# Where a skewed weight unit begins: 128 and 192 bytes behind a multiple of 256 in place of 64

## The reference

```python
for l in range(DEPTH):                       # first block
    proj = x @ w_in[l]                       # 1024 x 8200
    # retention, and an mLSTM on convolved q and k, each gated and projected
    mix = (gate_a * y_ret + gate_b * y_ml) @ w_out[l]
    x = _layer_norm(DEEPNORM_ALPHA * x + mix, ln1_g[l], ln1_b[l])
    gu = x @ w_gate_up[l]                    # 1024 x 5632
    hidden = jax.nn.silu(gu[..., :D_FF]) * gu[..., D_FF:]
    x = _layer_norm(DEEPNORM_ALPHA * x + hidden @ w_down[l], ln2_g[l], ln2_b[l])
for l in range(DEPTH):                       # second block
    proj = rms_norm(x) @ w_in_2[l]           # 1024 x 3584
    # dilated attention, a gated linear recurrence, stick-breaking attention
    x = x + y @ w_out_2[l]
```

## Time and profile before

| | |
|---|---|
| median of 3 runs | 1157.38 us (1156.76 to 1159.45) |
| profiled execution, its time | 1157.0 us |
| profiled execution, its span | 1155.2 us |
| TensorE busy with matmuls | 1142.6 us, 99% |
| VectorE, ScalarE busy | 67%, 50% |
| mean DMA rate | 183 GB/s |
| clock granted to TensorE in the 40 slices of the page | full in all |

### The profile page before, as it was taken

One profiled execution on the slowest core, in us unless ns is written; L12 is line 12 of the kernel. 1 busy time (PEld: TensorE's weight loads), 2 busy tenths in 40 slices (PEclk: granted clock), 3 DMA queues, 4 the chain that ended last, 5 costly groups with the idle time before them and its releaser, 6 DMA issues.

```text
span 1155.2 us, 18539 instructions
## 1 busy us (share of the span) xinstructions
PE 1142.6 (99%) x7762; PEld 1039.4 (90%) x7762; DVE 772.9 (67%) x1056; ACT 577.2 (50%) x668; POOL 28.8 (2%) x36
## 2 busy tenths in 40 slices
PE   9999999999999999999999999999999999999997
PEld 7989998998999988999998898899988789978996
DVE  5887866667655546697774667755555766885676
ACT  6565445433544434454544544444443456745663
POOL 0000000001000000000000000000000100010000
PEclk9999999999999999999999999999999999999999
DMA  8764455556656463745455556765556363346320
GB/s 298 272 218 147 163 202 175 191 184 210 223 186 214 162 206 113 249 152 183 140 189 182 183 183 218 232 206 179 187 201 216 139 219 124 133 146 245 128 93 37
DMA packets 130098, 211.62 MB, mean 183 GB/s; under 512 B 6624, under 2 KB 52704, under 8 KB 129888
## 3 DMA queue, kind: packets, MB, share of 16 engines
q1 hardware_dynamic: 128272, 204.15, 52.5%
q0 software_dynamic: 1744, 6.29, 1.7%
HBM read 209.37 MB, written 1.05 MB: 182 GB/s over the span
## 4 chain that ended last, share of the span: by engine, by line
PE 89%; ACT 4%; DVE 3%; issue 2%; DMA 1%; SPq 1%; POOL 0%; POOLq 0%; DVEq 0%; ACTq 0%
PE ps L513 87%; DMA raw<-in_w_in 1%; ACT wh L999 1%; DVE wl L1430 1%; PE ps L740 1%; PE ps L646 1%; PE ps L840 0%; ACT L1038 0%; SPq L447 0%; POOL small L468 0%; ACT L1041 0%; DVE xl L1524 0%; ACT ee L1317 0%; PE ps L822 0%; DVE zz L1996 0%
## 5 line engine op out<-in xcount | busy, mean ns | idle before, releaser
L1430 DVE TENSOR_TENSOR wl<-raw,wh 128x2048 fp32r<-128x2048 f32 (+1 forms) x186 | 415.0, 2237 | 167.0 <-ACT wh L999 166.7
L999 ACT ACTIVATE wh<-raw 128x2048 fp32r<-128x2048 f32 (+1 forms) x190 | 358.4, 1892 | 184.3 <-PE ps L513 162.4
L513 PE MATMUL ps<-xh,wh 128*128 128x256 f32 x1328 | 370.4, 279 | 1.5 <-issue 1.5
L513 PE MATMUL ps<-xl,wh 128*128 128x256 f32 x1328 | 367.2, 277 | 0.0
L513 PE MATMUL ps<-xh,wl 128*128 128x256 f32 x1312 | 363.4, 277 | 0.0
L513 PEld LDWEIGHTS ps<-xh,wh 128*128 128x128 f32 x1328 | 249.7, 188 | 4.7 <-issue 4.1
L513 PEld LDWEIGHTS ps<-xl,wh 128*128 128x128 f32 x1328 | 249.9, 188 | 0.2
L513 PEld LDWEIGHTS ps<-xh,wl 128*128 128x128 f32 x1312 | 246.7, 188 | 0.0
L513 PE MATMUL ps<-wh,xh 128*128 128x512 f32 (+1 forms) x440 | 171.4, 390 | 2.6 <-DVE xl L1524 1.6
L513 PE MATMUL ps<-wh,xl 128*128 128x512 f32 (+1 forms) x440 | 168.3, 383 | 0.0
L513 PE MATMUL ps<-wl,xh 128*128 128x512 f32 (+1 forms) x440 | 168.1, 382 | 0.0
(11 more groups left out here) (303 smaller groups left out, 1471.8 us busy)
## 6 DMA issues: line engine op xcount, KB each, us to landing
raw<-in_w_in SPq DMA_DIRECT2D x89, 1024.0 KB, 4.9
raw<-in_w_gate_up SPq DMA_DIRECT2D x88, 512.0 KB, 4.8
raw<-in_w_down SPq DMA_DIRECT2D x20, 1024.0 KB, 4.8
raw<-in_w_out SPq DMA_DIRECT2D x16, 1024.0 KB, 4.8
raw<-in_w_proj_ret SPq DMA_DIRECT2D x8, 1024.0 KB, 4.8
raw<-in_w_proj_mlstm SPq DMA_DIRECT2D x8, 1024.0 KB, 4.8
rows<-in_ln_g POOLq DMA_DIRECT2D x4, 512.0 KB, 4.2
rows<-in_ln_b POOLq DMA_DIRECT2D x4, 512.0 KB, 5.7
```

What stands on the lines that cost most here:

```text
L513: return pe.matmul(o, a, b, start=start, stop=False, skip_group_check=True)
L999: act.activation(stretch(wh, u, 0, m), source(u)[:, 0:m], ACT.Copy).then_inc(s_hi, 1)
L1430: dve.tensor_tensor(stretch(wl, u, a, nk * n), source(u)[:, a:nk * n], f32(stretch(wh, u, a, nk * n)), ALU.subtract).then_inc(s_lo, 1 if a ...
```

## The change

The constant `APART = (32, 48)` gives a skew for each layer. Every unit that was skewed by 16 floats (64 bytes) is skewed by 32 floats (128 bytes) in layer 0 and by 48 floats (192 bytes) in layer 1, in both blocks. Column 3072 of `w_in_2`, which is the unit of cvg, had no skew and gets the same one. Nothing else differs: no instruction, wait, transfer or buffer is added or moved.

```diff
+APART = (32, 48)
...
         for c0 in (3072, 3584, 1024, 1536, 0, 512, 6152, 6664, 7176, 7688, 2048, 2560, 5120, 5632):
-            cols(w, c0, 512, SKEW if c0 in (3072, 3584, 0, 512, 6152, 6664, 7176, 7688) else 0)
-        for name, skew in (("w_proj_ret", SKEW), ("w_proj_mlstm", SKEW), ("w_out", 0)):
+            cols(w, c0, 512, APART[l] if c0 in (3072, 3584, 0, 512, 6152, 6664, 7176, 7688) else 0)
+        for name, skew in (("w_proj_ret", APART[l]), ("w_proj_mlstm", APART[l]), ("w_out", 0)):
...
-                                      (g[:, k0:k0 + KU, FF + 256 * j:FF + 256 * j + 256], 256, 256)], SKEW if j > 1 else 0))
+                                      (g[:, k0:k0 + KU, FF + 256 * j:FF + 256 * j + 256], 256, 256)], APART[l] if j > 1 else 0))
...
         for c0 in (0, 512, 1024, 1536, 2560, 2048, 3072):
-            cols(A["w_in_2"][l], c0, 512, SKEW if c0 in (1536, 2560, 2048) else 0)
+            cols(A["w_in_2"][l], c0, 512, APART[l] if c0 in (1536, 2560, 2048, 3072) else 0)
```

## The result

The changed kernel took 1175.37 us (median of 4 runs, 1175.06 to 1175.65) beside 1157.42 us for the kernel before in the same runs. The ratio is 1.0155, 95% interval 1.0143 to 1.0167. The forecast was 1156.2 us with a range of 1153.3 to 1166.0, so the time lies above the range, and it moved the other way than forecast.

A forecast was written before the change was run, and what follows sets the result against it. The prediction took TensorE to bound the kernel, as matmul count by step from start to start. Its four terms, -1.2 + 0 + 0 + 0 us, took the median 1157.4 to 1156.2 us, range 1153.3 to 1166.0.

The forecast's parts named there:

- the floor: Fastest steady step of 256-column matmuls on TensorE, 113.3 ns from start to start, which no skew was to lower.
- Step (1): Skewed 256-column stages: half of 522 slow steps near 117.8 ns return to 113.3 ns, -1.2 us.
- the catches: Stretches of skewed matmuls entered at a slow pace of 117.8 ns that then holds; 522 steps, 2.3 us in all.
- The bounds of (1): Pace of the skewed stages: the floor of 113.3 ns from below, the unskewed 120.0 ns from above.
- The rival with both layers caught: Every skewed step of both layers at 117.8 ns, 1175 us; part of a rival with chance 0.18.
- Step (2): First few slow steps behind each interruption of skewed stages: 0 forecast, at best -0.7 us.
- Step (3): cvg's newly skewed unit: 1.25 us less TensorE work, hidden by ScalarE and VectorE work, so 0 forecast.
- Step (4): ScalarE and VectorE on shifted slots: L1430 2291 to 2295 ns skewed, 2282 unskewed; 0 forecast.
- The catch spreads: Skewed steps go to 117.8 ns: 7.9 us in block one for one layer, 1166.3 us total; chance 0.18.
- 128 as bad as 0: Pattern repeats at 128 bytes, so layer 0 runs at 120.0 ns throughout, 1171.3 us; chance 0.12.
- Everything pays: All slow stretches and slow beginnings go and cvg's saving is exposed, 1153.1 us; chance 0.10.
- Nothing happens: Distance matters only as zero or not zero, with cvg's saving hidden, 1157.4 us; chance 0.10.

## Why the prediction was wrong, step by step

**The bound and the floor: right.** No stretch in any of the fourteen kernels ran below 113.3 ns, and all 18 us came through the step.

**Step (1), the skewed stages: wrong, and it alone decides.** It put the catches at -1.2 us, "half of them gone", "because the step from 0 to 64 bytes took the pace from always 120 to mostly 113.3, and a larger distance needs a larger slip". That made a direction out of two points. Measured: 18.2 us more in place of 1.2 less. The pace isn't monotone in the distance; 80 bytes is already slow, and of the distances tried only 64 and 192 were ever seen at 113.3 ns, 64 in most stretches and 192 in few. What was right in it is that a pace "belongs to how a stretch is entered, and it then holds"; the step stopped short of asking which distances have a free pace to enter at all (128 has none) and which have one but seldom find it (192).

**The bounds of (1): right, the range wrong.** All steady paces that were measured lie between 113.3 and 120.0 ns. The rival with both layers caught gave 1175 us, which is the time measured, but in part by luck: layer 0 of the first block cost 2.0 us more than the 7.9 it had (a pace of 118.7 and not 117.8 ns), and layer 1 cost 1.4 us less (free stretches). The range stopped at one layer, on the ground that "nine tenths escape now". That counts escapes at 64 bytes only and says nothing of 128 or 192. With two distances that no row showed, both ends belonged in the range.

**Step (2), beginnings: can't be read apart** after the change, since most stages no longer reach the floor. **Step (3), cvg hidden: right**, shown by the run with cvg alone (ratio 1.0001, wait for yl 0.2 to 0.9 us) and by the chain's 29.39 us before and after. The mechanism that I gave, side work of ScalarE and VectorE, is what the chain shows. **Step (4), L1430: right**, 2293 ns. But its reading was not: the 2282 ns is that of `wls`, a spare buffer that one unit alone uses, and the other unskewed units of that window have a median of 2292 ns, so skew made no difference that this line shows. The skewed units are 100, not some 120. In the kernel before:

```profile
L1430 DVE TENSOR_TENSOR wl<-raw,wh x9: 1224/2292/2293, 850.6 to 888.7; 128x2048 fp32r<-128x2048 f32 x8, 128x1024 fp32r<-128x1024 f32 x1
```

**The rivals.** *The catch spreads*, which had a chance of 0.18, was the right one in place and near in size: 7.9 us forecast for a layer at 117.8 ns, 6.5 measured in layer 1, where some stretches stayed free, and 9.9 in layer 0, where the pace is 118.7. *128 as bad as 0* is wrong in its ground, a period of 128 bytes: 192 did not behave like 64, and the long stretch at 128 has 118.7 ns; that some stretches at 128 have 120.0 ns it had right. *Everything pays* is wrong: no catch was saved, and cvg's saving stayed hidden. *Nothing happens* is wrong: the step is up to 6.7 ns longer than 113.3 by distance alone. The Trainium skill (TensorE: Matmul & The Clock Gate, Part 2: What happens when you issue a matmul) says that loading the next weights takes no SBUF read bandwidth from the running matmul. That all distances would then be alike does not agree with the runs; whether it is read bandwidth that the 6.7 ns go to, no run here shows.

**Open.** Why 64 bytes is good for 256 columns and 0 for 512, and what in a restart decides between 113.3 and 117.8 ns. The kernel with only cvg's unit changed shows that it isn't the operands alone: the first half of mqk0, the same instructions on the same addresses, was caught there (117.8 ns) and free in the kernel before. It was caught in the same way in two more kernels that don't differ up to there, that with ff2 to ff10 changed and that with the 512-column stages skewed. First the kernel before, then that with cvg changed:

```profile
L513 PE MATMUL ps<-xh,wh 128*128 128x256 f32 x14 | 3.9, 276 | 0.0
...
L513 PE MATMUL ps<-xh,wh 128*128 128x256 f32 x14 | 3.9, 281 | 0.0
```
I didn't try distances between 48 and 80 bytes other than 64.

## What to carry to other kernels

Where TensorE is the bound and loads a new stationary operand for each matmul, as here, the distance modulo 256 bytes between stationary and moving operand is a tuning parameter; in this kernel it was worth up to 6% of the step (120.0 against 113.3 ns); measure each candidate, for each number of moving columns, and don't interpolate. Read it from the step between starts in a long stretch without interruption, and look at short stretches too, since one distance can have several paces; one kernel can test a different distance in each stage. Before you forecast a move to a value that no row shows, let the range reach to the worst row you have.

## What the hardware showed that I had not expected

- A pace is handed on. At 192 bytes ff4 to ff10 ran at 113.3 ns behind two stages at 64 bytes, and at 117.8 ns without them; at 64 bytes three stages stayed at 117.8 ns behind stages at 0.
- One load of three at a bad distance slows all three kinds of step: 118.2 ns in the mean with only the low part at 128 bytes, 118.7 with all.
- At 128 bytes the pace is no single step but a cycle of five, from 115 to 122 ns, with a mean of 118.7; in ff2 to ff10 at 0 every step is 120 ns.
- The good distance depends on the form: 64 bytes for 256 moving columns (113.3 against 120.0 ns at 0), 0 for 512 (226.6 against 233.3 ns at 64), of the distances tried.
- The modelled duration of a matmul doesn't tell paces apart: 281 ns stood for steps of 117.8 and of 118.7 ns, 283 and 285 for steps of 120.0.
